# A decoder step on one core: the rows between gate/up and down turned by VectorE instead of TensorE

## The reference

```
g_sel = argmax(h @ w_rg + b_rg)                       # 1 of 4 groups
top_v, top_i = top_k(e_logits of that group, 2)       # 2 of its 8 experts
gate = p_g * softmax(top_v)
for each of 32 experts e, x = its tokens (1024 wide):
    y = (silu(x @ w_eg[e]) * (x @ w_eu[e])) @ w_ed[e] # 1024 -> 512 -> 1024
out[token] += gate * y
result = layer_norm(ALPHA * h + out)
```

## Time and profile before

| | |
|---|---|
| time, median of 3 runs | 1114.95 us (1112.65 to 1116.19) |
| profiled execution, its own time | 1115.75 us |
| its span | 1113.8 us |
| granted TensorE clock over the span | 0.963 |
| PE busy | 1049.3 us (94%) |
| DVE busy | 586.9 us (53%) |
| DMA | 293.30 MB, mean 263 GB/s |

### The profile page before, as it was taken

The page is one execution under the profiler, slowest core; times in us unless marked ns, Lnnn a source line. Parts: engine busy times, 40 slices in busy tenths (PEclk is TensorE's granted clock), DMA queues, the critical chain, the costliest instruction groups (busy, mean ns, idle before and its releaser), DMA issues. The chain is left out here.

```text
span 1113.8 us, 20740 instructions
## 1 busy us (share of the span) xinstructions
PE 1049.3 (94%) x8280; PEld 662.4 (59%) x8280; DVE 586.9 (53%) x1281; ACT 213.0 (19%) x364; POOL 210.5 (19%) x193
## 2 busy tenths in 40 slices
PE   9999999999999899995999999999999999989980
PEld 8999998999997686454443344344344333434430
DVE  2799999800026722476455654554454453535425
ACT  3322311222225630001001101110110110101013
POOL 2444430232210011012002112111111211110110
PEclk9999999999898999996899999999999999989995
DMA  8468724146424426531989999999999999999724
GB/s 296 161 255 315 297 78 161 69 159 198 146 85 161 180 67 253 193 111 50 350 333 407 395 391 400 396 386 393 389 389 380 389 393 351 365 353 350 268 55 163
DMA packets 45680, 293.30 MB, mean 263 GB/s; under 512 B 11519, under 2 KB 15231, under 8 KB 26173
## 3 DMA queue, kind: packets, MB, share of 16 engines
q1 hardware_dynamic: 22285, 163.96, 38.2%
q10 hardware_dynamic: 12624, 102.63, 22.7%
q0 software_dynamic: 10720, 25.98, 7.9%
HBM read 286.83 MB, written 41.12 MB: 294 GB/s over the span
## 5 line engine op out<-in xcount | busy, mean ns | idle before, releaser
L1752 DVE STREAM_TRANSPOSE scratch<-x_columns 32x256 f32<-32x256 f32 x384 | 166.7, 434 | 8.0 <-DMA x_columns<-h_rows,token_rows 2.0
L1423 DVE SCALAR_TENSOR_TENSOR z_conv_gates<-scratch,column_vectors,z_conv_gates 128x512 f32<-128x512 f32 x240 | 142.9, 672 | 0.0
L1762 DVE SCALAR_TENSOR_TENSOR x_columns<-ps,column_vectors,x_columns 128x256 f32<-128x256 f32 x32 | 15.5, 484 | 219.0 <-ACT x_columns L1304 205.8
L989 PE MATMUL ps<-region_b,scratch 128*64 128x512 f32 x496 | 115.6, 616 | 8.9 <-DMA region_b<-in_gate_up_rows 8.9
L989 PE MATMUL ps<-region_a,scratch 128*64 128x512 f32 x528 | 119.3, 601 | 2.3 <-DVE scratch L1752 1.5
L1030 PE MATMUL ps<-z_conv_gates,x_columns 128*64 128x512 f32 x512 | 116.9, 598 | 0.0
L588 PE MATMUL ps<-z_split,region_b_split 128*128 128x272 f32 x384 | 111.2, 290 | 0.0
L586 PE MATMUL ps<-z_split,region_b_split 128*128 128x272 f32 x384 | 110.8, 289 | 0.1
L587 PE MATMUL ps<-z_split,region_b_split 128*128 128x272 f32 x384 | 110.4, 287 | 0.0
L989 PEld LDWEIGHTS ps<-region_a,scratch 128*64 128x64 f32 x528 | 38.6, 138 | 73.7 <-issue 71.2
L1870 POOL TENSOR_TENSOR region_b_split<-region_b,region_b_split 128x1024 fp32r<-128x1024 f32 x24 | 64.4, 2700 | 88.0 <-ACT region_b_split L1103 88.0
(11 more groups left out here) (278 smaller groups left out, 1441.0 us busy)
## 6 DMA issues: line engine op xcount, KB each, us to landing
region_b<-in_gate_up_rows SPq DMA_DIRECT2D x21, 2048.0 KB, 29.7
region_a<-in_gate_up_rows ACTq DMA_DIRECT2D x21, 2048.0 KB
z_conv_gates<-in_down_rows SPq DMA_DIRECT2D x32, 1024.0 KB, 12.6
z_conv_gates<-in_down_rows ACTq DMA_DIRECT2D x32, 1024.0 KB, 31.3
region_a<-in_gate_up_rows SPq DMA_DIRECT2D x12, 2048.0 KB
region_b<-in_w_in_pairs SPq DMA_DIRECT2D x20, 1024.0 KB, 4.9
region_b<-in_gate_up_rows ACTq DMA_DIRECT2D x10, 2048.0 KB, 29.9
region_b<-in_cache_tiles POOLq DMA_DIRECT2D x16, 768.0 KB, 4.9
```

Of the source, the lines that this page charges most:

```text
L989: last = pe.matmul(ps[half * BIG:(half + 1) * BIG, 2, :], ecols_big[s][:, 4 * c + k, :], w[:, k, half, :], start=c + k == 0, stop=c + k == 4)
L1423: ve.scalar_tensor_tensor(dst, win(k), wdw_c[:, bass.ds(k * CT + c, 1)], dst, ALU.mult, ALU.add).then_inc(conv_step, 1)
L1752: last = ve.transpose(out, xg[s][r * R:(r + 1) * R, q * QD:(q + 1) * QD].rearrange("p (k c) -> p k c", k=KD))
```

## The change

The three transposes on TensorE, the PSUM tile `hid_ps`, its semaphore `hid_turned` and VectorE's copy go away. VectorE's new `turn_hidden(e)` turns the hidden rows from SBUF to SBUF in 32 by 32 blocks: eight instructions of 32 partitions x 128 columns for the big rows, each of which reads one quarter of partitions and writes another (or the same), and one of 128 x 128 for the rest rows. Since only blocks are turned, the order of the 512 hidden columns over partitions and steps differs, and the host lays out the down weights by that order; the size and shape of their transfers stay. `down` reads `hcols_big` by step k alone. The wait for the down product of e-1 (`dn_big_ps`) stands now ahead of all nine instructions, and `multiply_big` waits for `hcols_sb` in place of `hid_turned`. The path for further blocks (more than 96 rows of one expert), which is not taken with these inputs, changes in the same way.

```diff
--- before.py
+++ after.py
@@ -314,9 +314,8 @@
         act_big, act_rest = xt_t[:, 3 * D:3 * D + 256], xt_t[:, 3 * D + 256:3 * D + 384]
         hid_big, hid_rest = xt_t[:, 3 * D + 384:3 * D + 640], xt_t[:, 3 * D + 640:3 * D + 768]
         hcols = xt_t[:, 3 * D + 768:3 * D + 1152]
-        hcols_big = hcols[:, 0:2 * P].rearrange("p (c h r) -> p c h r", c=2, h=2)
-        hcols_rest = hcols[:, 2 * P:3 * P].rearrange("p (j r) -> p j r", j=GROUPS)
-        hid_ps = ps[:, 4, 0:3 * P]
+        hcols_big = hcols[:, 0:2 * P].rearrange("p (k r) -> p k r", k=KF)
+        hcols_rest = hcols[:, 2 * P:3 * P].rearrange("p (k r) -> p k r", k=KF)
         gates_at = ps[:, 7, 256:256 + 2 * NE].rearrange("p (two e) -> p two e", two=2)
         over_at = ps[:, 7, 320:320 + 3 * OVER].rearrange("p (n b) -> p n b", n=3)
 
@@ -368,8 +367,8 @@
         scattered = [sem(f"scattered{s}") for s in range(SLOTS)]
         idx_set_e, xgt_sb, big_ps, rest_ps, big_act, rest_act, big_hid, rest_hid = (
             sem(x) for x in ("idx_copied", "xgt_sb", "big_ps", "rest_ps", "big_act", "rest_act", "big_hid", "rest_hid"))
-        hid_turned, hcols_sb, dn_rest_ps, dn_big_ps, yo_big, yo_rest = (
-            sem(x) for x in ("hid_turned", "hcols_sb", "down_rest_ps", "down_big_ps", "yo_big", "yo_rest"))
+        hcols_sb, dn_rest_ps, dn_big_ps, yo_big, yo_rest = (
+            sem(x) for x in ("hcols_sb", "down_rest_ps", "down_big_ps", "yo_big", "yo_rest"))
         ov_load = sem("ov_load")
         over_done = sem("over_done")
         fin_loaded = [sem(f"fin_loaded{t}") for t in range(NTT)]
@@ -1004,13 +1003,6 @@
                                              ecols_rest[s][:, 4 * c + k, :], w[:, k, j // 2, :, n0:n0 + P], start=c + k == 0, stop=c + k == 4)
                 last.then_inc(rest_ps, 1)
 
-            def turn_hidden(e):
-                pe.wait_ge(big_hid, e + 1)
-                for c in range(2):
-                    pe.transpose(hid_ps[:, c * P:(c + 1) * P], hid_big[:, c * P:(c + 1) * P], eye)
-                pe.wait_ge(rest_hid, e + 1)
-                pe.transpose(hid_ps[:, 2 * P:3 * P], hid_rest, eye).then_inc(hid_turned, 1)
-
             def down(e, weights, ready):
 
                 w = weights.rearrange("p (k d) -> p k d", k=KF)
@@ -1027,7 +1019,7 @@
                     pe.wait_ge(yo_big, e)
                 for k in range(KF):
                     for half in range(2):
-                        last = pe.matmul(ps[half * BIG:(half + 1) * BIG, 5, :], hcols_big[:, k % 2, k // 2, :], w[:, k, half * 512:(half + 1) * 512],
+                        last = pe.matmul(ps[half * BIG:(half + 1) * BIG, 5, :], hcols_big[:, k, :], w[:, k, half * 512:(half + 1) * 512],
                                          start=k == 0, stop=k == KF - 1)
                 last.then_inc(dn_big_ps, 1)
 
@@ -1043,7 +1035,6 @@
                 before_s = (s + 2) % SLOTS
                 gates_of(e, s, rounds)
                 rows_of(e - 1, before_s, rounds - (s == 0))
-                turn_hidden(e)
 
             def keep_running(n):
 
@@ -1053,7 +1044,6 @@
             pe.wait_ge(idx_set, 1)
             keep_running(20)
             gates_of(0, 0, 1)
-            turn_hidden(0)
             expert(1, 1, 1)
             expert(2, 2, 1)
             with pe.Fori(LOOP.start // 3, LOOP.stop // 3) as i:
@@ -1077,7 +1067,6 @@
                     pe.wait_ge(ov_load, 64 * i + 64)
                     gate_up_big(i + NE, 0, gu_place[1], lambda c: None)
                     gate_up_rest(i + NE, 0, gu_place[1])
-                    turn_hidden(i + NE)
                     down(i + NE, dn_place[1], lambda: None)
 
 
@@ -1758,7 +1747,7 @@
             def multiply_big(e):
                 ve.wait_ge(big_act, e + 1)
                 if not (isinstance(e, int) and e == 0):
-                    ve.wait_ge(hid_turned, e)
+                    ve.wait_ge(hcols_sb, e)
                 ve.scalar_tensor_tensor(hid_big, ps[:, 2, 256:512], gate_big[:, column_of(e)], act_big, ALU.mult, ALU.mult).then_inc(big_hid, 1)
 
             def multiply_rest(e):
@@ -1773,11 +1762,18 @@
                     last = ve.tensor_copy(yo[s][BIG:BLK, j * 256:(j + 1) * 256], ps[j * REST:(j + 1) * REST, 6, 0:256])
                 last.then_inc(yo_rest, 1)
 
-            def hidden_copy(e):
-                ve.wait_ge(hid_turned, e + 1)
+            def turn_hidden(e):
                 if not (isinstance(e, int) and e == 0):
                     ve.wait_ge(dn_big_ps, e)
-                ve.tensor_copy(hcols, hid_ps).then_inc(hcols_sb, 1)
+                ve.wait_ge(big_hid, e + 1)
+                for half in range(2):
+                    for g in range(2):
+                        rows = slice((2 * half + g) * R, (2 * half + g + 1) * R)
+                        for u in range(2):
+                            part = slice((2 * half + u) * R, (2 * half + u + 1) * R)
+                            ve.transpose(hcols_big[part, :, g * R:(g + 1) * R], hid_big[rows, u * P:(u + 1) * P].rearrange("p (k c) -> p k c", k=KF))
+                ve.wait_ge(rest_hid, e + 1)
+                ve.transpose(hcols[:, 2 * P:3 * P], hid_rest).then_inc(hcols_sb, 1)
 
             def expert(e, s, before, gathers):
 
@@ -1793,7 +1789,7 @@
                     rows_back(e - 1, last_s, before)
                 if gathers is not None:
                     turn_rows(e + 1, next_s, 2)
-                hidden_copy(e)
+                turn_hidden(e)
 
             ve.wait_ge(gathered[0], 16)
             for r in range(RB):
@@ -1831,7 +1827,7 @@
                         turn_rows(i + NE, 0, r)
                     multiply_big(i + NE)
                     multiply_rest(i + NE)
-                    hidden_copy(i + NE)
+                    turn_hidden(i + NE)
                     rows_back(i + NE, 0, i + SLOT_USES[0])
 
 
@@ -2029,7 +2025,7 @@
     tiles = np.concatenate(tiles)
     gate_up = np.stack([inputs[n][0].reshape(NE, GROUPS, 2, KD // 2, R, 2, FE // 2) for n in ("w_expert_gate", "w_expert_up")], 6)
     gate_up = gate_up.transpose(0, 2, 1, 4, 3, 5, 6, 7).reshape(NE, 2, P, KD * FE)
-    down = inputs["w_expert_down"][0].reshape(NE, KF, P, D).transpose(0, 2, 1, 3).reshape(NE, P, KF * D)
+    down = inputs["w_expert_down"][0].reshape(NE, GROUPS, KF, R, D).transpose(0, 1, 3, 2, 4).reshape(NE, P, KF * D)
     return {"gate_up_rows": gate_up, "down_rows": down, "cache_tiles": tiles, "x_columns": x.reshape(N, KD, P).transpose(2, 1, 0).reshape(P, KD * N), "w_in_pairs": w_in, "columns": columns, "state_columns": state}
```

## The result

| | before | after |
|---|---|---|
| time, median | 1114.97 us (1112.44 to 1118.25, 20 runs) | 1117.44 us (1114.43 to 1122.3, 20 runs) |
| profiled execution, its own time | 1115.75 us | 1115.38 us |
| its span | 1113.8 us | 1113.6 us |
| PE busy | 1049.3 us | 1028.6 us |
| DVE busy | 586.9 us | 656.4 us |

The ratio is 1.003, 95% interval 1.002 to 1.004: some 2.5 us slower, small but clear of no change. The profiled execution lies at the low end of its 20 runs, so the traces must be compared stretch by stretch.

A forecast was written before the change was run, and what follows sets the result against it. Transfers, paced by a few slow DMA engines, were taken to bound the loop, although TensorE was full too. Profiled 1115.75 + 0 (loop) + 1.7 (end) + 1.6 (clock) = 1119.05, less 0.80: 1118.2 us predicted, range 1113 to 1122.5.

The forecast's parts named there:

- within 0.3%: Case for the whole kernel: time between the borders 1111.6 and 1118.3 us, chance 0.46.
- +1.6 us for the clock: End of the loop: TensorE's 2.8 us pause lowers the clock in down of 31, +1.6 us, bounds 0 and +2.8.
- The loop is held by landings, the transposes are worth nothing in it: Expert loop: weights land 17.93 us apart, TensorE wants 16.40, so its saved time becomes waits; 0 us.
- TensorE is the bound: Rival, expert loop: landings follow issues, 14.9 us are gained, 1103.4 us; chance 0.10, whole or in part.
- 0.48 us an expert leave TensorE: Expert loop: removing three transposes shortens TensorE's period from 16.40 to 15.92 us, about 14.9 us over 31 periods.
- some 20: Sign in the expert loop: waits for gate/up weights at nearly every expert after about 16, some 20 us in sum.
- Nine transposes in 2.7 us, free in the loop: VectorE, expert loop: nine transposes at 0.302 us each, 2.7 us, covered by idle time, so nothing in the loop.
- +1.7 us at the end: After down of 30: the nine transposes stand uncovered before down of 31, +1.7 us, bounds +1.0 and +2.9.
- the clock does not fall: Rival, end of the loop: no clock loss after the pause, 1116.7 us; chance 0.22.
- the rival of falls in the last phases: Rival, gate/up of experts 30 or 31: clock falls add 1.7 to 3.4 us, 1121 us; 0.26, including engines slowed further.
- A few slow DMA engines hold the pace.: Weight transfers in the expert loop: a few uneven, slow engines set 17.93 us for 6 MiB.

The follow-up runs named there:

- after_again: Experiment 1: the changed kernel, unedited, timed again beside the kernel before: 1116.65 us, ratio 1.0022.
- own_buffer: Changed kernel with a separate buffer for expert 31's hidden columns, turned without waiting for down of 30: 1113.48 us, ratio 0.9996.
- filled_pause: Experiment 3: changed kernel with twelve unused matmuls filling TensorE's pause between down of 30 and down of 31: 1116.6 us, ratio 1.0024.
- copy_for_turn: Changed kernel with the nine transposes replaced by one copy of the unturned rows (wrong products): 1115.17 us, ratio 1.0003.
- both pairs with free transfers: Kernel before and changed kernel, with half the down weights not loaded: 1099.19 and 1083.02 us; with filled rows spread over the block: 1096.85 and 1082.52 us.
- less_down_after: Changed kernel with half of the down weights not loaded and the loaded half used twice: 1083.02 us, ratio 0.970.
- spread_after: Changed kernel with each expert's filled rows spread over its block of 96: 1082.52 us, ratio 0.9699 to the kernel before.
- no_scatter: Changed kernel with the scatters of the experts' results left out: 1076.87 us, ratio 0.9654 to the kernel before.
- spread_own: Changed kernel with spread rows and a separate buffer for expert 31's hidden columns: 1077.0 us, ratio 0.9645 to the kernel before.

## Why the prediction came out as it did

The forecast was 1118.2 us and "within 0.3%" the likeliest; 1117.44 us and 1.003 came. That the number came within 0.8 us is in part luck: one of its two terms, +1.6 us for the clock, was not there, and the measured loss holds some 0.5 to 0.7 us that the other does not account for. By its steps:

**The loop is held by landings, the transposes are worth nothing in it.** Right, and shown: gate/up of expert 31 at 521.5 us from the loop's start against 521.6 (522.1, 521.8, 522.1 and 522.7 in after_again, own_buffer, filled_pause and copy_for_turn); copy_for_turn at 1.0003; both pairs with free transfers 16.2 and 14.3 us apart. The landing of expert 29's weights in after, against the earlier trace rows:

```profile
L486 SPq DMA_DIRECT2D region_b<-in_gate_up_rows x1: 333/333/333, 982.3 to 982.3; - x1
...
DMA to landing us min/median/max: 41.7/41.7/41.8
```

and of expert 5's:

```profile
L1241 ACTq DMA_DIRECT2D region_b<-in_gate_up_rows x1: 353/353/353, 578.3 to 578.3; - x1
...
DMA to landing us min/median/max: 15.5/15.6/15.8
```

That is 982.3 + 41.8 = 1024.1 less 578.3 + 15.8 = 594.1, over 24 experts 17.92 us apart, as foretold (17.93). The rival "TensorE is the bound", at 0.10, is out.

**0.48 us an expert leave TensorE.** Too small: the period fell by 0.63. The 0.48 was from the start of the transposes to the next matmul. The other 0.15 lies beside them: from the start of down's big part to what follows it 3.48 us instead of 3.58 (709.50 - 706.02 against 717.25 - 713.67), and from the start of gate/up's big part to its rest rows 6.97 instead of 7.02. These matmuls follow each other more closely without a transpose in between; why was not tested. The first wait for weights came at expert 15 instead of about 17, also because the loop began 2 us earlier with less lead, and the waits were 24.9 us instead of "some 20". It moved no time, since the loop was not TensorE's.

**Nine transposes in 2.7 us, free in the loop.** Right. By line and form from 560 to 1050 us:

```profile
L1774 DVE STREAM_TRANSPOSE x_columns<-x_columns 32x128 f32<-32x128 f32 x232 | 70.2, 303 | 3.7
...
L1776 DVE STREAM_TRANSPOSE x_columns<-x_columns 128x128 f32<-128x128 f32 x29 | 9.0, 312 | 0.4
```

303 ns for 302 expected from the step of the multiplies in the earlier trace rows. No wait of TensorE for `hcols` appears in the loop. The big multiply still had 1.86 us of idle time ahead of it at the least, near the 2.0 that follow from the forecast's terms (4.63 less 0.48 less 2.2). One reading was off, to the safe side: the gate/up phase behind the earlier trace rows starts at 717.73 and not at 717.25, so its big part lasts to 724.8 and not to 724.3.

The Trainium skill, "VectorE: DVE Perf Modes", section "Rules for kernel authors", gives 128 x 128 transposes to TensorE and 32 x 32 ones within a bank to VectorE. This kernel turns 32 x 32 blocks, some of them into another quarter of the partitions, and lays out the weights to match; it has no 128 x 128 transpose left. So the rule does not speak against the change, as the prediction had it. Where TensorE is the bound, in less_down_after and spread_after, the change was worth 16 and 14 us.

**+1.7 us at the end.** Right in size: 1.81 in the profile. own_buffer takes it away and the old pause with it.

**+1.6 us for the clock in down 31.** This term failed. The clock stayed at 1.00 in down 31 after 2.95 us, in all five profiles that have that pause (after, after_again, less_down_after, no_scatter, spread_after), and filling the pause (experiment 3) changed nothing. The premise was wrong that a length of pause next to one that brought a fall brings one too. The rival "the clock does not fall" (0.22) had the mechanism: 1116.7 us, with 1116.65 measured in after_again and 1117.44 in the first comparison.

**What stays open.** Measured are +2.3 and +2.5 us, accounted for are 1.8, which lies within the interval of experiment 1 (from 1.0 us) and just under that of the first comparison (from 2.2 us). The loop may hold the rest: with TensorE's transposes gone, expert 31 came 0.1 us earlier to 1.1 us later than in before, counted from the loop's start, but of before there is one profile only. In after_again the cause of 0.5 us of it is seen, a fall of the clock at expert 30; that is the rival of falls in the last phases (0.26), in small. The 20 times of after lie in two heaps, 1114.4 to 1117.7 and 1119.1 to 1122.3, and the upper was not explained: no profile of an execution of the upper heap exists. Besides those falls (the first profile of after has one 8.78 us phase at 1024.13, the third from the last) it may come from ahead of the loop: gate/up of expert 0 starts at 536.8 us in the first profile of after and at 538.6 in after_again, the same kernel, and anywhere from 534.2 to 539.8 over the twelve profiled executions.

**"A few slow DMA engines hold the pace."** Right as to the effect, as far as the runs can tell: 17.92 us between landings became 16.3 with the scatters left out and, at the same bytes, 16.25 with the rows spread. The reason lay in this kernel, in where the rows lie; that it works through single engines is inferred. The prediction also drew on the sentence on engines 7 and 15 in the Trainium skill, "DMA: Bandwidth & Descriptors", section "Latency and other measured facts". No run here names an engine, so whether these two were among the slow ones is not shown.

## What to carry to other kernels

When a queue's time to landing grows along a loop, compare landing to landing, not the engines' busy shares. If that interval is longer than the compute engine's period and the lead is used up before the loop ends, it is the bound, and work taken off the full compute engine turns into waits. If the DMA share dips while a transfer is outstanding, look for indirect transfers whose filled rows lie together, and try to spread them. After that, price the same change again: here it went from a loss of 0.3% to a gain of 14 us. And look at the last turn of the loop, where a step that is covered everywhere else stands bare.

## What the hardware showed that was not expected

- Small indirect transfers can slow large plain ones by where their rows lie: landing of 2 MiB in 33.8 us with the filled rows first, in 12.9 us with them spread. That every engine carries six neighbouring rows of the 96 was only the theory behind the step of six places; the trace names no engines, and no other spread was run, so any other order that parts the filled rows might do as well.
- Length alone does not tell whether a pause brings the clock down. Phases of 32 matmuls after it took 8.78 us (clock fell, to 0.50 for a 2 us slice) or 7.09 (it did not). It fell after 1.49 us in before and 1.99 and 3.14 in after; it did not after 1.60 in before, 1.80 and, ahead of down 31, 2.95 in after, and 2.87 in after_again. At the same place of the program 2.60 us did it in spread_after and 2.59 did not in spread_own. One fall costs 1.69 us. In the middle of a loop held by landings the next wait takes it up; at expert 30, in after_again, 0.5 us of it was left.
